# Attention rounds of a decoder trunk: the value products move into the following round

## The chip, the cores and the metric

One core of a Trainium2 chip runs the whole program. The metric is the time of one execution on the device, in microseconds (us), smaller being better.

## What is computed

Two layers of a decoder trunk on 256 tokens of width 1024. Of each layer only the first half matters here: a combined projection and, among other branches, two kinds of attention on its columns.

```python
z = h @ w_in[l] + b_in[l]                       # 8448 columns
# branch A: 16 query heads, 4 key/value heads, window 128, a sink per head
oa = banded_attention(qa, ka, va, A_WINDOW - 1, sinks)
# branch C: 4 heads in each of 3 dilation groups, combined by their softmax weights
oc = sum_g softmax(lse)_g * dilated_group(qc_g, kc_g, vc_g)
merged = gate_a * (oa @ w_proj_a) + gate_b * (ob @ w_proj_b) + gate_c * (oc @ w_proj_c)
x = x + merged @ w_out
x = x + hier_moe(rms_norm(x), ...)              # expert stage, 32 experts
```

## The kernel before, in words

The engines' programs are written out by hand; each engine works through its own list in order and waits on semaphores. The trunk stage of a layer runs `z` as 17 column chunks of 512 (the last 256), each in four items, called convs and numbered j: conv j multiplies two of the eight 128-deep blocks of `h` with their weights, in three passes (high and low parts), 12 matmuls (L1488 to L1490). ScalarE casts the high part of a weight item (`high_at`, L933), VectorE subtracts the low part (`low_half`, L1140), SP loads the items. A chunk's sums stand in two banks, one for each block of 128 tokens, and VectorE adds the bias and copies them out (`z_out`, L1159).

The attention lies between the convs 44 to 67, so that TensorE always has work. It has 12 batches: b below 8 are two query heads of branch A each, b from 8 to 11 are the three groups' heads of branch C. A round b of TensorE (the loop at L1689) holds:

- `gates_conv(44 + 2b)`, into banks 6 and 7
- `scores(b + 1)` (L1611), which VectorE masks and takes the maximum of (`softmax_in`, L1254) and ScalarE turns into exponentials (`exps`, L1016); VectorE divides (`softmax_out`, L1291)
- `pv(b)`: `turn_probs(b)` transposes the probabilities (L1623), then `gates_conv(45 + 2b)`, then the products with the values: `product_pair(b)` (L1639) for b below 8, `products(b)` (L1656) for b = 9, which does batches 8 and 9; nothing for b = 8 and 10. Batch 11's products come later, outside the loop
- `qk(b + 2)`: transposes of the next queries and keys (L1592), where the batch needs new ones: none in rounds 7 and 9

ScalarE's round: `high_at(46 + 2b)`, `pv_out(b)` (L1030, turned probabilities out of banks 3 and 4), `exps(b + 1)`, `o_out(b)` (L1035, the products out of bank 5 into the place of the used queries), `qk_out(b + 2)` (L1009), `high_at(47 + 2b)`. Every product block writes bank 5 and waits until the one before it has been copied out (`o_evac`).

A round with odd b ends a chunk: conv 45 + 2b is its last, and the next conv starts a chunk in the same banks 6 and 7. Its first matmuls for each token block therefore wait for that block's copy on VectorE (`z_evac`); the chunk's convs do token block 1 (bank 7) first, and VectorE can take bank 7 while bank 6 is being finished (`z_half`). For b = 7 and 9 a small reduction (`group_max`) stands between the two copies:

```python
z_out(6, c, BANK, c + 1, True, (1,))
if b + 1 >= 8:
    group_max(b + 1)
z_out(6, c, BANK, c + 1, True, (0,))
low_half(46 + 2 * b, BANK if b < 9 else TAIL, 47 + 2 * b, 1)
```

Of the kernel before, what the change touches and what calls it, by code (L numbers as in the profile page):

```python
# [78 lines left out]
def trunk_program(nc, x, positions, norm1_g, w_in, b_in, attn_sinks, sgu_ln_g, sgu_ln_b, w_spatial,  # L79
# [7 lines left out]
    with ExitStack() as whole:  # L87
# [557 lines left out]
        def trunk_stage(l):  # L645
            with ExitStack():
# [4 lines left out]
                BATCHES = 12  # L651
# [21 lines left out]
                def ring_landed(slot, item):  # L673

                    return 16 * (item // 4 + 1 + (slot == 0 and item >= 40))


                def heads(b):
                    return 2 if b < 8 else 3

                def turned_before(b):

                    return 2 * b if b < 8 else 16 + 3 * (b - 8)
# [5 lines left out]
                def t_first(kind, b):  # L689


                    n = sum(qk_banks(i) for i in range(b if kind == "qk" else min(b + 2, BATCHES)))
                    return n + turned_before(max(b - 1, 0) if kind == "qk" else b)
# [20 lines left out]
                def pts_at(u):  # L714

                    return u % 3 if u < 16 else (u - 16) % 6
# [5 lines left out]
                with ExitStack():  # L722
# [189 lines left out]
                    def _(act):  # L912
# [8 lines left out]
                        def high(jj, w, landed, used):  # L921

                            if landed is not None:
                                act.wait_ge(ring_in[(jj // 2) % RING], landed)
                            if used is not None:
                                act.wait_ge(conv_used, used)
                            elif jj >= 64:
                                item_used(act, jj - 2)
                            if jj >= NARROW:
                                act.copy(whi[:, jj % 2, :].rearrange("p (k n) -> p k n", k=4),  # L930
                                         narrow_slot(jj, None)).then_inc(hi_ready, 1)
                                return
                            act.copy(whi[:, jj % 2, 0:2 * w], half_slot(jj, w)).then_inc(hi_ready, 1)  # L933
# [48 lines left out]
                        def high_at(j):  # L982
                            if j >= NARROW:
                                item = NARROW // 2 + j % 2
                                act.wait_ge(ring_in[item % RING], ring_landed(item % RING, item))
                                high(j, BANK, None, None)
                                return
                            high(j, TAIL if 64 <= j < Z_CONV else BANK, ring_landed(j // 2 % RING, j // 2), j - 1 if j < 64 else None)
# [33 lines left out]
                        def pv_out(b):  # L1022
                            for i in range(heads(b)):
                                t, u = t_first("pv", b) + i, turned_before(b) + i
                                act.wait_ge(t_ready, t + 1)
                                if 3 <= u < 19:
                                    act.wait_ge(pv_mm, u - 2 if u < 16 else 16)
                                elif u >= 22:
                                    act.wait_ge(pv_mm, 22)
                                act.copy(pts[:, pts_at(u), :], ps[:, 3 + t % 2, 0:384]).then_inc(t_evac, 1)  # L1030

                        def o_out(b):
                            for p in pairs_of(b):
                                act.wait_ge(pv_mm, turned_before(b + 1))
                                act.copy(o_at(p, 1), ps[:, 5, 0:S].rearrange("p (t c) -> p t c", t=TB)).then_inc(o_evac, 1)  # L1035
# [23 lines left out]
                        for b in range(BATCHES):  # L1059
                            if b == 7:  # L1060
                                halves_at(60)
                            else:
                                high_at(46 + 2 * b)
                            if b == BATCHES - 1:
                                high_at(47 + 2 * b)
                            pv_out(b)
                            if b == 8:
                                qk_out(b + 2, 0, 1)
                            if b == BATCHES - 2:
                                high_at(47 + 2 * b)  # L1070
                            if b + 1 < BATCHES:
                                exps(b + 1)
                            if b < BATCHES - 1:
                                o_out(b)
                            if b + 2 < BATCHES:
                                qk_out(b + 2, 1 if b == 8 else 0)
                            if b < BATCHES - 2:
                                high_at(47 + 2 * b)
                            if b in SPLITS:
                                o_high(SPLITS.index(b))  # L1080
# [377 lines left out]
                    def _(pe):  # L1458
# [103 lines left out]
                        def gates_conv(j, between=None):  # L1562

                            z_conv(j, 6, TAIL if j >= 4 * CHUNKS else BANK, j + 1, between, (1, 0),
                                   2 * (j // 4) if j > 4 * AHEAD else None)
# [32 lines left out]
                        def scores(b):  # L1598
                            src = b if b < 8 else 8 + 2 * ((b - 8) // 2)
                            if src >= 8:  # L1600
                                turn_taken(t_first("qk", src) + 1)
                            turn_taken(t_first("qk", src) + qk_banks(src) - 1)
                            if b >= 1:
                                pe.wait_ge(s_free, b)

                            for i, tb in SIDE_BY_SIDE[0:2 * heads(b)]:
                                r = HD * (i if b < 8 else (b + i) % 2)
                                rows = slice(r, r + HD)
                                q = qkt[rows, b % 2, 0:S] if b < 8 else qkt[rows, i, 0:S]
                                k = qkt[rows, 0 if b < 8 else i, S:2 * S]  # L1610
                                mm = pe.matmul(ps[:, i, tb * P:tb * P + (tb + 1) * P], q[:, tb * P:(tb + 1) * P],  # L1611
                                               k[:, 0:(tb + 1) * P], start=True, stop=True)
                                if tb:
                                    mm.then_inc(s_ready, 1)

                        def turn_probs(b, *which):
                            pe.wait_ge(p_ready, 2 * b + 1)
                            for c in range(3):
                                if c == 1:
                                    pe.wait_ge(p_ready, 2 * b + 2)  # L1620
                                for i in which:
                                    bank = bank_for(t_first("pv", b) + i)
                                    mm = pe.transpose(ps[:, bank, c * P:(c + 1) * P],  # L1623
                                                      probs[:, b % 2, i, c * P:(c + 1) * P], ident[:])
                                    if c == 2:
                                        mm.then_inc(t_ready, 1)
# [34 lines left out]
                        def pv(b, between=None):  # L1661
                            if between:
                                turn_probs(b, 0)
                                between()
                                turn_probs(b, 1)
                            else:
                                turn_probs(b, 0, 1)
                            gates_conv(45 + 2 * b, (lambda: turn_probs(b, 2)) if b >= 8 else None)
                            if b < 8:
                                product_pair(b)  # L1670
                            elif b % 2:
                                products(b)
# [16 lines left out]
                        for b in range(BATCHES - 1):  # L1689
                            gates_conv(44 + 2 * b, (lambda: qk(b + 1, 2, 3)) if qk_banks(b + 1) == 3 else None)  # L1690
                            if b == 0:
                                pe.wait_ge(z_evac, 2 * AHEAD)
                                qk(1)
                                pv(b, lambda: scores(1))
                            else:
                                scores(b + 1)
                                pv(b)
                            if b + 2 < BATCHES:
                                qk(b + 2)
# [927 lines left out]
```

## Time and profile before

| what | value |
|---|---|
| median of 3 runs | 1018.7 us (1018.06 to 1020.11) |
| profiled execution | 1018.59 us, its span 1016.9 us |
| mean granted TensorE clock of that span | 0.985 |
| busy in the span: TensorE, VectorE, ScalarE | 951.8, 560.8, 431.0 us |
| attention rounds | about 128 to 230 us and 630 to 732 us |

The span runs from the first to the last instruction. Engines: PE is TensorE's matmul, PEld its weight loads, DVE VectorE, ACT ScalarE. Matmuls are pipelined, and the ends of their records are modelled; distances between their starts are what a block costs.

### The profile page before, as it was taken

What the parts mean: (1) busy time and instruction counts of PE and PEld (TensorE: products, weight loads), DVE (VectorE), ACT (ScalarE), POOL (GpSimd) and SP (SyncE); (2) the same over time, 40 slices, a digit from 0 to 9 for tenths busy, and PEclk for the clock granted to TensorE, in tenths of its full rate; (3) what the DMA queues carried; (4) which work ended last, traced back from release to release, by engine and by line L of the source; (5) the groups of instructions that cost most, each with busy time, mean ns of one, the idle gap of its engine ahead of it and who ended that gap; (6) DMA issues with size and microseconds to landing.
All of it is one profiled execution on the core that took longest, in us unless ns stands there. A gap on an engine that the chain in (4) does not pass through costs nothing.

```text
span 1016.9 us, 15601 instructions
## 1 busy us (share of the span) xinstructions
PE 951.8 (94%) x5898; PEld 665.8 (65%) x5898; DVE 560.8 (55%) x1328; ACT 431.0 (42%) x920; POOL 58.6 (6%) x74
## 2 busy tenths in 40 slices
PE   9999999999999995976999999999999999977787
PEld 7888877778886441532588888777888954434333
DVE  7666787786883332220276668788868634122212
ACT  5434666766444120210363455666764441111122
POOL 1120400000010000000003004000000100000000
PEclk9999999999999998998999999999999999999989
DMA  9975644248999999999997756342599999999996
GB/s 351 348 244 191 193 138 125 83 123 321 361 391 398 422 426 423 426 427 426 418 392 239 239 180 201 125 125 64 174 355 345 406 418 413 425 425 425 426 427 273
DMA packets 97114, 313.03 MB, mean 308 GB/s; under 512 B 13424, under 2 KB 18576, under 8 KB 74512
## 3 DMA queue, kind: packets, MB, share of 16 engines
q1 hardware_dynamic: 96704, 312.04, 80.3%
q8 instruction: 44, 0.72, 0.3%
q14 instruction: 30, 0.25, 0.1%
q10 hardware_dynamic: 336, 0.02, 0.0%
HBM read 310.20 MB, written 1.84 MB: 307 GB/s over the span
## 4 chain that ended last, share of the span: by engine, by line
PE 76%; DMA 13%; SPq 7%; DVE 2%; ACT 1%; issue 1%; POOL 0%; DVEq 0%; POOLq 0%
PE ps L1488 16%; PE ps L1490 15%; PE ps L1489 15%; SPq L505 7%; PE ps L2154 6%; DMA arena<-in_w_expert_up_dram 5%; DMA arena<-in_w_expert_gate_dram 3%; DMA ring_rest<-in_w_expert_up_dram 3%; DMA ring_rest<-in_w_expert_down_dram 3%; PE ps L2128 2%; PE ps L1611 2%; PE ps L1513 2%; PE ps L2228 2%; PE ps L1623 2%; PE ps L2240 2%; PE ps L2099 1%
## 5 line engine op out<-in xcount | busy, mean ns | idle before, releaser
L1140 DVE TENSOR_TENSOR split_w<-arena,split_w 128x512 fp32r<-128x512 f32 (+1 forms) x352 | 232.9, 700 | 101.1 <-ACT split_w L933 97.6
L1488 PE MATMUL ps<-split_w,split_a 128*128 128x512 f32 (+1 forms) x736 | 283.9, 386 | 0.1
L1490 PE MATMUL ps<-split_w,split_a 128*128 128x512 f32 (+1 forms) x736 | 277.1, 376 | 0.0
L1489 PE MATMUL ps<-split_w,split_a 128*128 128x512 f32 (+1 forms) x736 | 276.7, 376 | 0.0
L933 ACT CAST split_w<-arena 128x1024 fp32r<-128x1024 f32 (+1 forms) x171 | 175.8, 1031 | 176.9 <-PE ps L1490 170.0
L1488 PEld LDWEIGHTS ps<-split_w,split_a 128*128 128x128 f32 x736 | 138.5, 188 | 26.6 <-issue 2.2
L1490 PEld LDWEIGHTS ps<-split_w,split_a 128*128 128x128 f32 x736 | 138.4, 188 | 26.0
L1489 PEld LDWEIGHTS ps<-split_w,split_a 128*128 128x128 f32 x736 | 138.7, 188 | 23.5
L2385 DVE SCALAR_TENSOR_TENSOR acts<-ps,wslot,acts 128x256 f32<-128x256 f32 x16 | 7.7, 483 | 171.6 <-ACT acts L2055 148.5
L2154 PE MATMUL ps<-arena,rows 128*32 128x512 f32 x416 | 90.0, 615 | 9.6 <-DMA arena<-in_w_expert_up_dram 6.9
L2154 PE MATMUL ps<-ring_rest,rows 128*32 128x512 f32 x352 | 76.0, 634 | 12.8 <-DMA arena<-in_w_expert_up_dram 12.8
L2055 ACT ACTIVATE acts<-ps,rslot 128x256 f32<-128x256 f32 x16 | 7.6, 474 | 154.0 <-PE ps L2154 149.6
L2128 PEld LDWEIGHTS ps<-arena,work 128*128 128x128 f32 x448 | 52.8, 197 | 28.8 <-issue 24.8
L2128 PE MATMUL ps<-arena,work 128*128 128x128 f32 x448 | 55.8, 283 | 15.6 <-issue 8.9
L2240 PE MATMUL ps<-rows,st 128*128 128x512 f32 x112 | 55.3, 617 | 0.9 <-DVE xs L2366 0.7
L1016 ACT ACTIVATE probs<-probs,neg 128x128 f32<-128x128 f32 x112 | 49.6, 444 | 10.4 <-DVE neg L1264 10.4
L1159 DVE SCALAR_TENSOR_TENSOR arena<-ps,rstd,arena 128x512 f32<-128x512 f32 (+2 forms) x68 | 47.1, 728 | 3.9 <-PE ps L1490 3.7
L2228 PE MATMUL ps<-arena,acts 128*32 128x512 f32 x272 | 43.6, 595 | 5.2 <-ACT acts L2059 5.2
L2154 PEld LDWEIGHTS ps<-arena,rows 128*32 128x32 f32 x416 | 23.6, 113 | 37.1 <-issue 37.0
L2154 PEld LDWEIGHTS ps<-ring_rest,rows 128*32 128x32 f32 x352 | 19.7, 116 | 42.6 <-issue 42.5
L2369 DVE TENSOR_TENSOR xs<-ps,xs 128x512 f32<-128x512 f32 x48 | 33.2, 691 | 18.2 <-PE ps L2240 18.2
L2240 PEld LDWEIGHTS ps<-rows,st 128*128 128x128 f32 x112 | 17.7, 189 | 30.5 <-issue 30.5
(284 smaller groups left out, 1074.6 us busy)
## 6 DMA issues: line engine op xcount, KB each, us to landing
arena<-in_w_in_dram SPq DMA_DIRECT2D x62, 1024.0 KB, 5.3
arena<-in_w_expert_down_dram SPq DMA_DIRECT2D x36, 1024.0 KB, 19.5
arena<-in_w_expert_gate_dram SPq DMA_DIRECT2D x34, 1024.0 KB, 23.9
arena<-in_w_expert_up_dram SPq DMA_DIRECT2D x32, 1024.0 KB, 24.0
ring_rest<-in_w_expert_down_dram SPq DMA_DIRECT2D x24, 1024.0 KB, 17.4
ring_rest<-in_w_expert_gate_dram SPq DMA_DIRECT2D x22, 1024.0 KB, 23.9
ring_rest<-in_w_expert_up_dram SPq DMA_DIRECT2D x22, 1024.0 KB, 25.5
arena<-in_w_proj_a_dram SPq DMA_DIRECT2D x8, 1024.0 KB, 5.1
```

Of the source, the lines that this page charges most:

```text
L505: sp.dma_start(slot, w[l, 4 * n + e].rearrange("(p k) f -> p (k f)", p=P)).then_inc(done, 16)
L933: act.copy(whi[:, jj % 2, 0:2 * w], half_slot(jj, w)).then_inc(hi_ready, 1)
L1016: act.activation(probs[:, i, n, lo:hi], probs[:, i, n, lo:hi], ACT.Exp, bias=neg[:, i, tb, n:n + 1], accum_out=den[:, i, tb, n:n + 1])
L1140: dve.tensor_tensor(wlo[:, jj % 2, cols], half_slot(jj, w)[:, cols], whi[:, jj % 2, cols].bitcast(F32), ALU.subtract).then_inc(low_split i ...
L1159: dve.scalar_tensor_tensor(out=z[:, tb, cols], in0=ps[:, bank + tb, 0:w], scalar=rstd[:, tb:tb + 1], in1=z[:, 0, cols], op0=ALU.mult, op1= ...
L1488: pe.matmul(o, hi, rhs_hi, start=first, stop=False)
L1489: pe.matmul(o, hi, rhs_lo, start=False, stop=False)
L1490: return pe.matmul(o, lo, rhs_hi, start=False, stop=last)
L2128: mm = pe.matmul(ps[:, 4 + k // 4, (k % 4) * QUAD:(k % 4 + 1) * QUAD], work[:, tb, k * P:(k + 1) * P], onehot[:, n % 2, tb, :], start=(tb ...
L2154: mm = pe.matmul(ps[e * EC:(e + 1) * EC, n % 2, :].rearrange("p (a f) -> p a f", a=2), xsel[:, k, e * EC:(e + 1) * EC], w, start=(k == 0), ...
L2228: mm = pe.matmul(ps[e * EC:(e + 1) * EC, 2 + nh, :], at_sb[:, kf, e * EC:(e + 1) * EC], w, start=(kf == 0), stop=(kf == 1), skip_group_che ...
L2240: pe.matmul(ps[:, 4 + tb, :], st[:, n % 2, tb * P:(tb + 1) * P], y[:, nh * BANK:(nh + 1) * BANK], start=True, stop=True).then_inc(R.back_r ...
```

## The change

The products of a batch are issued in the following round, directly behind that round's scores and ahead of its turned probabilities. ScalarE copies bank 5 out ahead of its copies of the turned probabilities of that round. Round 0 has no products, round 8 has pair 7, round 10 the products of batches 8 and 9.

```diff
--- before.py
+++ after.py
@@ -1063,6 +1063,8 @@
                                 high_at(46 + 2 * b)
                             if b == BATCHES - 1:
                                 high_at(47 + 2 * b)
+                            if b >= 1:
+                                o_out(b - 1)
                             pv_out(b)
                             if b == 8:
                                 qk_out(b + 2, 0, 1)
@@ -1070,8 +1072,6 @@
                                 high_at(47 + 2 * b)
                             if b + 1 < BATCHES:
                                 exps(b + 1)
-                            if b < BATCHES - 1:
-                                o_out(b)
                             if b + 2 < BATCHES:
                                 qk_out(b + 2, 1 if b == 8 else 0)
                             if b < BATCHES - 2:
@@ -1666,6 +1666,8 @@
                             else:
                                 turn_probs(b, 0, 1)
                             gates_conv(45 + 2 * b, (lambda: turn_probs(b, 2)) if b >= 8 else None)
+
+                        def products_of(b):
                             if b < 8:
                                 product_pair(b)
                             elif b % 2:
@@ -1694,6 +1696,7 @@
                                 pv(b, lambda: scores(1))
                             else:
                                 scores(b + 1)
+                                products_of(b - 1)
                                 pv(b)
                             if b + 2 < BATCHES:
                                 qk(b + 2)
```

## Rows read from the trace of the kernel before

**Rows 1.** The page: the chain that ended last, shares of the span by engine.
```profile
PE 76%; DMA 13%; SPq 7%; DVE 2%; ACT 1%; issue 1%; POOL 0%; DVEq 0%; POOLq 0%
```

**Rows 2.** Table of stages, round 2: stretch, length, busy and count per engine, clock, DMA.
```profile
152.30:160.90 8.60, 8.60 (x51) 6.36 (x51) 6.37 (x20) 5.78 (x15) 0.00 (x0) 1.00 0.40 124
```

**Rows 3.** Timeline of TensorE, round 2: start, length, engine, line, operation, operands, count.
```profile
152.30 0.93 PE L1611 MATMUL ps<-qkt 64*128 64x128 f32 x8
153.16 0.87 PE L1623 MATMUL ps<-ident,probs 128*128 128x128 f32 x6
153.79 0.48 PE L1488 MATMUL ps<-split_w,split_a 128*128 128x512 f32 x1
...
156.41 0.39 PE L1490 MATMUL ps<-split_w,split_a 128*128 128x512 f32 x1
156.73 0.87 PE L1639 MATMUL ps<-mixed,arena 128*64 128x256 f32 x8
157.53 0.33 PE L1592 MATMUL ps<-ident,arena 128*128 128x128 f32 x1
...
157.94 0.49 PE L1488 MATMUL ps<-split_w,split_a 128*128 128x512 f32 x1
```

**Rows 4.** Timeline of TensorE: transposes of batch 0 directly behind conv 41.
```profile
124.87 0.39 PE L1490 MATMUL ps<-split_w,split_a 128*128 128x512 f32 x1
125.10 0.27 PE L1592 MATMUL ps<-ident,arena 128*128 128x128 f32 x1
...
125.45 0.48 PE L1488 MATMUL ps<-split_w,split_a 128*128 128x512 f32 x1
```

**Rows 5.** The chain of waits: scores of three heads, start and time on the chain.
```profile
195.75 1.50 PE ps L1611 x12
```

**Rows 6.** Timeline of ScalarE and VectorE, round 2: brackets hold the wait before.
```profile
157.67 0.37 ACT L1035 COPY arena<-ps 128x256 f32<-128x256 f32 x1 [0.63 <-PE ps L1639]
159.79 1.29 DVE L1140 TENSOR_TENSOR split_w<-arena,split_w 128x512 fp32r<-128x512 f32 x2 [1.28 <-ACT split_w L933]
```

**Rows 7.** Timeline, end of round 1: VectorE's two copies, TensorE's conv 47 and 48.
```profile
147.80 1.43 DVE L1159 SCALAR_TENSOR_TENSOR arena<-ps,rstd,arena 128x512 f32<-128x512 f32 x2 [0.55 <-PE ps L1490]
148.06 0.39 PE L1490 MATMUL ps<-split_w,split_a 128*128 128x512 f32 x1
149.37 0.48 PE L1488 MATMUL ps<-split_w,split_a 128*128 128x512 f32 x1
```

**Rows 8.** Timeline, end of round 7: the two copies, and conv 59 and 60.
```profile
200.24 0.74 DVE L1159 SCALAR_TENSOR_TENSOR arena<-ps,rstd,arena 128x512 f32<-128x512 f32 x1
200.46 0.39 PE L1490 MATMUL ps<-split_w,split_a 128*128 128x512 f32 x1
201.16 0.74 DVE L1159 SCALAR_TENSOR_TENSOR arena<-ps,rstd,arena 128x512 f32<-128x512 f32 x1
201.57 0.50 PE L1488 MATMUL ps<-split_w,split_a 128*128 128x512 f32 x1
```

**Rows 9.** Timeline, round 9: a weight load that waits for VectorE's division.
```profile
215.16 0.95 DVE L1291 TENSOR_TENSOR probs<-probs,den 128x768 f32<-128x768 f32 x1
216.17 0.42 PEld L1623 LDWEIGHTS ps<-ident,probs 128*128 128x128 f32 x4 [0.39 <-DVE probs L1291]
```

**Rows 10.** Timeline, end of round 9 and conv 64: copies, products, conv, scores.
```profile
219.51 0.75 DVE L1159 SCALAR_TENSOR_TENSOR arena<-ps,rstd,arena 128x512 f32<-128x512 f32 x1
220.10 2.17 PE L1656 MATMUL ps<-mixed,arena 128*64 128x256 f32 x24
220.45 0.74 DVE L1159 SCALAR_TENSOR_TENSOR arena<-ps,rstd,arena 128x512 f32<-128x512 f32 x1
222.21 0.38 PE L1488 MATMUL ps<-split_w,split_a 128*128 128x256 f32 x1
222.67 0.28 PE L1488 MATMUL ps<-split_w,split_a 128*128 128x256 f32 x1
223.83 1.57 PE L1611 MATMUL ps<-qkt 64*128 64x128 f32 x12
```

## The prediction

> **What bounds the kernel now.** I read four views, in this order. The page's chain of waits says who sets the end: TensorE holds 76% of it, DMA 13% [rows 1]. The table of stages, cut at the starts of the score blocks, says that in the attention rounds TensorE is busy for the whole of a round (8.60 of 8.60 us in round 2) at a granted clock of 1.00 (2.4 GHz), while VectorE has 6.37 and ScalarE 5.78 us of work [rows 2]. So a round costs what TensorE's queue costs, plus what TensorE waits for. The timeline of TensorE then gives the price of each block, start to start, and that of VectorE gives the moments at which banks 6 and 7 come free. All rounds of one parity look alike and layer 2 repeats layer 1, so a few rows stand for all.
>
> **Prices of the blocks** (round 2) [rows 3]: scores 0.86 (152.30 to 153.16), turned probabilities 0.63 (to 153.79), product pair 0.80 (156.73 to 157.53), four transposes for the next queries and keys 0.41 (to 157.94). The products begin 0.32 after the start of the last projection matmul (156.41 to 156.73). Where transposes follow a projection block directly, the step is only 0.23 and four of them take 0.35 [rows 4].
>
> **The change, part by part.** It adds and removes no instruction. It moves nine blocks of products per layer (pairs 0 to 7 and the three-head block issued for batch 9) from the end of their round to the place between the scores and the turned probabilities of the next round; and nine copies of bank 5 on ScalarE, from behind the exponentials to ahead of the copies of the turned probabilities. SP's and POOL's queues are untouched; their waits are on counts that this order reaches in the same sequence.
>
> *Transitions on TensorE.* No row shows scores followed by products. Nearest are scores followed by full-array transposes, which have the 0.86, and products followed by them, which have the 0.80 [rows 3]. I take both unchanged. At the old place the projection block now runs straight into the transposes: 0.32 becomes 0.23 and 0.41 becomes 0.35, a gain of 0.15 in a round that has them.
> Bounds of the unknown step: a score block of three heads holds the chain 1.50 [rows 5] and one of two 0.86, so a third head alone costs about 0.64 and two side by side would cost that as well if nothing drained; the drain behind scores is then about 0.21. The new step can save that 0.21 (no second drain) or pay it twice. Over 18 places that is -3.8 to +3.8 us; I take 0, as the rows nearest by kind have it, and half of it on each side for the range.
> The Trainium skill (TensorEngine Tiling (Array Packing), Key Properties) says that changing the tiling mode drains TensorE. By it a round has four such changes before (into and out of scores, into and out of products) and three after, one fewer; the entries on which this shows cost 0.09 here [rows 3, 4], which is in the sum already; at the 0.21 estimated for a drain behind scores the 18 places would give back another 2.2 us.
>
> *Round 0* issues no products any more: -0.80 and -0.15.
>
> *Rounds 2, 4, 6* exchange one pair for the other: -0.15 each, -0.45. For ScalarE: the copy of bank 5 waited 0.63 for the products, behind the exponentials [rows 6]; now it and the two copies of the turned probabilities stand ahead of them and the exponentials end about 0.6 later. That lies beside TensorE's next block; VectorE waited 1.28 there for the next weight half [rows 6], which ScalarE still casts at the same distance from the transposes. Were that cover gone, each such round would pay what exceeds it.
>
> *Rounds 1, 3, 5*: here the next projection block starts a new column chunk in banks 6 and 7, which VectorE must have emptied. Its two copies start at 147.80 and the following block at 149.37 [rows 7]: the products (0.80) and two transposes stood between. In the new order the whole projection block, and so the first copy, comes 0.80 later: 148.60, plus 0.74 for one copy [rows 8], is 149.34. A weight load that waits for VectorE starts 0.06 after its end (215.16 + 0.95 = 216.11, then 216.17) [rows 9], so 149.40, where the clean order would give about 149.25 (148.06 + 0.80 + 0.23 + two transposes at 0.09). The second copy ends 0.7 later, the second stationary group needs it 0.8 later: not late. So these rounds lose what they gained: +0.05 each, +0.15.
>
> *Round 7* has no transposes at its end, so the new chunk would follow at once: 200.46 + 0.80 + 0.23 = 201.49. The copies, 0.92 apart because a small maximum stands between them [rows 8], come: first 201.00 to 201.74 (it waits for the matmul 0.69 ahead of the last, 199.77 + 0.80 + 0.39), so TensorE starts at 201.80; second 201.92 to 202.66, so the second group starts at 202.72 instead of the natural 202.58. Before, that group followed the start at 201.57 by 0.78, at 202.35; the block ends 0.4 later than before: +0.40, where the clean order had won 0.2.
>
> *Round 8* receives pair 7: +0.80.
>
> *Round 9* loses the three-head products, 2.11 (220.10 to 222.21), and has again no transposes. The clean start of the next block is 220.10 - 0.32 + 0.23 = 220.01. VectorE's copies begin at 219.51 and 220.45 [rows 10]; they don't move, since products no longer precede this block in its round. First free at 219.51 + 0.74 + 0.06 = 220.31, second at 220.45 + 0.74 + 0.06 = 221.25. Before, the second group started at 222.67 and the scores 1.16 later, at 223.83 [rows 10]. After: 221.30 + 1.16 = 222.46, -1.37. Of the 2.11 taken away, some 0.9 comes back as waiting.
>
> *Round 10* receives the three-head products: +2.11. Behind it each step keeps its distance from the projection block: the turned probabilities of batch 11 still come at their old distance.
>
> **Sum per layer**: -0.95 + 0.15 - 0.45 + 0.40 + 0.80 - 1.37 + 2.11 = +0.69; two layers +1.4 us. The profiled execution took 1018.6 us (span 1016.9 and 1.7 around it), the median of three runs is 1018.7, so no correction is due. Forecast: 1018.6 + 1.4 = 1020.0. About 0.2% (2.0 us) is what a measurement of this kernel can tell from no change; the forecast is inside it. The late trunk and the expert stage I take as shifted whole: their loads wait for counts behind this stage.
>
> **Rivals.**
> 1. *The bank waits don't bind*, for instance because VectorE gets to its copies sooner than I shift them. Then nine places save 0.15 in each layer, 2.7 us, 1015.9: faster. For it: most rounds have VectorE a fourth idle [rows 2]. Against: in rounds 7 and 9 the copies have a fixed order with the maximum between them and nothing in the change hastens them. Chance 0.12, with the cheaper drain counted in.
> 2. *Two drains in a row* (slower). The products wait for the scores to leave the array and the transposes for the products, and the first of these costs more than 0.86 includes. Place: between scores and products, 18 times. At the full 0.21 extra it costs 3.8 us, 1023.8. It decides from 0.035 each ((2.04 - 1.4) / 18). For it: every change between block kinds shows a step longer than its stream. Against: the 0.86 already holds the drain of the scores, and the 0.80 that of the products. Chance 0.26.
> 3. *ScalarE's order becomes the bound* (slower): exponentials 0.6 later, then the next weight half late by what exceeds the 1.28; 0.3 in each of five rounds and both layers is 3 us on top of the forecast, 1023.0. Against: ScalarE does 5.78 of 8.60 us, and the wait removed (0.63) pays for the 0.6. Chance 0.07.
> 4. *The change moves nothing that counts*: the expert stage takes up the shift, 1018.6. For it: DMA has 13% of the chain [rows 1]. Against: its loads start on counts that shift too. Chance 0.10.
>
> **How the numbers follow.** Forecast 0.45. Rivals 1 to 4 as given. The forecast and rival 4 are inside 0.2%: 0.55. Faster 0.12, slower 0.33. The range takes half of the drain bound (1.9) around the forecast and reaches toward both other sides: 1017.0 to 1022.8.
>
> **What would show it.** In the timeline of the changed kernel: products right behind scores at 0.86, and turned probabilities 0.80 behind those; transposes 0.23 behind the last projection matmul; the blocks behind rounds 7 and 9 waiting on VectorE's copy out of banks 6 and 7, in sum about 0.5 and 0.9 us per layer; round 2 at 8.45, round 9 at about 8.4 instead of 9.76. It is wrong if scores to products is over 0.95 or under 0.75, if those waits are missing, or if ScalarE's weight casts become late.

## Result and profile after

The changed kernel takes 1020.57 us in the median of 11 runs, the kernel before 1018.31 us (12 runs): ratio 1.0019, 95% interval 1.0011 to 1.0027, a loss of 1.1 to 2.8 us. A twelfth run of the changed kernel was a slow one of 1922.65 us and is in none of these figures. The forecast was 1020.0, a loss of 1.4 us; measured are about 2 us.

The page of the changed kernel, its span, TensorE's row, and the chain by engine:

```profile
span 1018.0 us, 15601 instructions
...
PE 957.5 (94%) x5898; PEld 669.7 (66%) x5898; DVE 560.4 (55%) x1328; ACT 430.5 (42%) x920; POOL 58.4 (6%) x74
...
PE 77%; DMA 10%; SPq 7%; DVE 3%; issue 1%; ACT 1%; DVEq 0%; POOL 0%; POOLq 0%
```

The number of instructions is unchanged, and beside TensorE's share of the chain VectorE's grew, from 2% [rows 1] to 3%. The spans of two single executions differ by 1.1 us, which is not the difference of the kernels: the changed one reached its first scores 0.54 us earlier (127.85 against 128.39), ahead of anything that was changed, and took about 0.4 us less between the two attention stages. So I measure inside the stage, from start to start of the score blocks, where single executions repeat within some 0.03 us a round.

The table of stages for rounds 1, 2, 7 and 9 of the changed kernel, columns as in [rows 2]:

```profile
142.44:150.95 8.51, 8.48 (x49) 6.24 (x48) 6.24 (x20) 5.45 (x15) 0.00 (x0) 1.00 0.37 123
150.95:159.41 8.46, 8.46 (x52) 6.44 (x51) 7.02 (x21) 5.77 (x15) 0.00 (x0) 1.00 0.39 126
194.23:203.56 9.33, 9.08 (x51) 6.48 (x50) 8.17 (x28) 6.82 (x21) 0.00 (x0) 1.00 0.21 58
213.88:222.30 8.42, 7.79 (x46) 5.76 (x45) 7.57 (x29) 5.81 (x20) 0.00 (x0) 1.00 0.50 133
```

In round 2 TensorE is still busy throughout; in rounds 7 and 9 it now has 0.25 and 0.63 us without a matmul, at the same granted clock of 1.00. The kernel before had none in round 7:

```profile
195.68:204.56 8.88, 8.88 (x51) 6.56 (x51) 7.67 (x28) 6.71 (x21) 0.00 (x0) 1.00 0.22 61
```

The lengths of all rounds of layer 1, taken from the timelines (us, start of scores(b + 1) to start of scores(b + 2); the last entry runs to the transposes of branch B behind the stage):

| round | 0 | 1 | 2 | 3 | 4 | 5 | 6 | 7 | 8 | 9 | 10 and on | sum |
|---|---|---|---|---|---|---|---|---|---|---|---|---|
| before | 8.28 | 8.35 | 8.60 | 8.35 | 8.60 | 8.36 | 9.47 | 8.88 | 9.51 | 9.76 | 18.73 | 106.89 |
| after | 7.31 | 8.51 | 8.46 | 8.51 | 8.45 | 8.52 | 9.34 | 9.33 | 10.32 | 8.42 | 20.84 | 108.01 |
| difference | -0.97 | +0.16 | -0.14 | +0.16 | -0.15 | +0.16 | -0.13 | +0.45 | +0.81 | -1.34 | +2.11 | +1.12 |
| predicted | -0.95 | +0.05 | -0.15 | +0.05 | -0.15 | +0.05 | -0.15 | +0.40 | +0.80 | -1.37 | +2.11 | +0.69 |

Layer 2 gives +0.99 in the same way (114.15 to 115.14 from its first scores on). Together +2.1 us: the whole difference lies in the two attention stages. Behind the second one the two profiled executions take the same, 272.50 and 272.47 us.

**The new order on TensorE**, round 2 of the changed kernel, timeline with the columns of [rows 3]:

```profile
150.95 0.93 PE L1611 MATMUL ps<-qkt 64*128 64x128 f32 x8
151.81 0.87 PE L1639 MATMUL ps<-mixed,arena 128*64 128x256 f32 x8
152.61 0.88 PE L1623 MATMUL ps<-ident,probs 128*128 128x128 f32 x6
153.24 0.49 PE L1488 MATMUL ps<-split_w,split_a 128*128 128x512 f32 x1
...
155.88 0.39 PE L1490 MATMUL ps<-split_w,split_a 128*128 128x512 f32 x1
156.11 0.27 PE L1592 MATMUL ps<-ident,arena 128*128 128x128 f32 x1
...
156.47 0.48 PE L1488 MATMUL ps<-split_w,split_a 128*128 128x512 f32 x1
```

The steps are 0.86, 0.80, 0.63, and then 0.23 and 0.36: the prices of [rows 3] and [rows 4] in a new sequence. Two changes of tiling in a row cost nothing beyond them.

**Where a chunk ends.** The end of round 1, with VectorE's two copies, to be held against [rows 7]:

```profile
147.11 1.44 DVE L1159 SCALAR_TENSOR_TENSOR arena<-ps,rstd,arena 128x512 f32<-128x512 f32 x2 [1.36 <-PE ps L1490]
147.37 0.39 PE L1490 MATMUL ps<-split_w,split_a 128*128 128x512 f32 x1
147.60 0.38 PE L1592 MATMUL ps<-ident,arena 128*128 128x128 f32 x2
148.01 0.47 PE L1488 MATMUL ps<-split_w,split_a 128*128 128x512 f32 x1
```

The block behind the two transposes starts 0.41 after the first of them. Two transposes take 0.20 behind products (149.17 to 149.37 in the kernel before) and 0.13 directly behind a projection block (649.72 to 649.85 in the kernel with short copies, below), so some 0.27 of it is waiting. The copy of bank 7 ends at 147.11 + 0.74 = 147.85, and the first matmul follows 0.16 later.

The end of round 7, against [rows 8]:

```profile
199.55 0.75 DVE L1159 SCALAR_TENSOR_TENSOR arena<-ps,rstd,arena 128x512 f32<-128x512 f32 x1 [0.68 <-PE ps L1490]
200.48 0.74 DVE L1159 SCALAR_TENSOR_TENSOR arena<-ps,rstd,arena 128x512 f32<-128x512 f32 x1
...
200.45 0.47 PE L1488 MATMUL ps<-split_w,split_a 128*128 128x512 f32 x1 [0.25 <-DVE arena L1159]
201.28 0.50 PE L1488 MATMUL ps<-split_w,split_a 128*128 128x512 f32 x1
201.62 0.39 PE L1489 MATMUL ps<-split_w,split_a 128*128 128x512 f32 x1
```

And of round 9, against [rows 10], where nothing stands between conv 63 and conv 64 any more:

```profile
219.30 0.75 DVE L1159 SCALAR_TENSOR_TENSOR arena<-ps,rstd,arena 128x512 f32<-128x512 f32 x1
219.56 0.40 PE L1490 MATMUL ps<-split_w,split_a 128*128 128x512 f32 x1
...
220.20 0.36 PE L1488 MATMUL ps<-split_w,split_a 128*128 128x256 f32 x1 [0.24 <-DVE arena L1159]
220.24 0.74 DVE L1159 SCALAR_TENSOR_TENSOR arena<-ps,rstd,arena 128x512 f32<-128x512 f32 x1
...
221.03 0.39 PE L1488 MATMUL ps<-split_w,split_a 128*128 128x256 f32 x1 [0.24 <-DVE arena L1159]
221.26 0.28 PE L1489 MATMUL ps<-split_w,split_a 128*128 128x256 f32 x1
```

Both token blocks wait for their bank. The brackets say 0.24 each, but the records' modelled ends hide part of it: by the starts, the first block comes 0.64 after the last matmul of conv 63 where 0.23 is the clean step, and the second 0.83 after the first where 0.46 was [rows 10]. The next matmul then comes 0.23 behind, where 0.12 is the clean step of these narrower blocks (222.67 to 222.79 in the kernel before): a restart behind this wait costs another 0.11. That is 0.41 + 0.37 + 0.11, about 0.9 us in this one place. Round 7 has the same 0.11 (201.28 to 201.62, clean 0.23). Before, TensorE had no wait for L1159 in the attention stage.

### The profile page after: what moved, and what is told of

The parts are those of the page before. It is cut to its first block, busy times and chain, and to the rows that moved or that the text cites. A ratio compares the mean times of both kernels' runs of the same rounds, so it can differ in the third digit from the quotient of the medians.

```text
span 1018.0 us, 15601 instructions
## 1 busy us (share of the span) xinstructions
PE 957.5 (94%) x5898; PEld 669.7 (66%) x5898; DVE 560.4 (55%) x1328; ACT 430.5 (42%) x920; POOL 58.4 (6%) x74
## 4 chain that ended last, share of the span: by engine, by line
PE 77%; DMA 10%; SPq 7%; DVE 3%; issue 1%; ACT 1%; DVEq 0%; POOL 0%; POOLq 0%
PE ps L1488 16%; PE ps L1490 15%; PE ps L1489 15%; SPq L505 7%; PE ps L2157 7%; DMA arena<-in_w_expert_up_dram 5%; DMA ring_rest<-in_w_expert_down_dram 5%; PE ps L2131 3%; PE ps L2231 3%; PE ps L2243 2%; PE ps L1611 2%; PE ps L1513 2%; PE ps L1623 2%; PE ps L2102 1%; PE ps L1639 1%
## 5 line engine op out<-in xcount | busy, mean ns | idle before, releaser
L2131 PEld LDWEIGHTS ps<-arena,work 128*128 128x128 f32 x448 | 56.4, 208 | 28.7 <-issue 24.6
L2131 PE MATMUL ps<-arena,work 128*128 128x128 f32 x448 | 59.3, 295 | 15.5 <-issue 8.7
L1159 DVE SCALAR_TENSOR_TENSOR arena<-ps,rstd,arena 128x512 f32<-128x512 f32 (+2 forms) x68 | 47.2, 728 | 10.1 <-PE ps L1490 9.9
L2405 DVE COPY rows<-ps 128x512 f32<-128x512 f32 x14 | 9.7, 692 | 52.4 <-PE ps L2231 52.4
```

The source lines that it names most:

```text
L1159: dve.scalar_tensor_tensor(out=z[:, tb, cols], in0=ps[:, bank + tb, 0:w], scalar=rstd[:, tb:tb + 1], in1=z[:, 0, cols], op0=ALU.mult, op1= ...
L2131: mm = pe.matmul(ps[:, 4 + k // 4, (k % 4) * QUAD:(k % 4 + 1) * QUAD], work[:, tb, k * P:(k + 1) * P], onehot[:, n % 2, tb, :], start=(tb ...
```

## Experiments

Theory W: TensorE waits for VectorE's copies out of banks 6 and 7, which the moved blocks had covered. Against it theory D, that back-to-back changes of tiling drain more, and theory S, that ScalarE's order or a shift in later stages is the cause.

**The change again.**

> The changed kernel again, beside the kernel before on one chip. Theory W (the bare bank copies: where a round ends a column chunk, TensorE's next projection block waits for VectorE's copies out of banks 6 and 7, and the moved products were what covered them): +2.2 us, ratio 1.002. Theory D (two drains in a row between scores, products and transposes) gives the same here and differs in the next runs.

1020.5 against 1018.45 us, ratio 1.0023 (1.0011 to 1.0035). Its rounds repeat those above: 115.29 and 115.24 us in the two layers, from their first scores to the transposes behind the stage, against 114.17 and 114.15 before. All stage times below are taken between these two points.

**Only the even batches move.** Line numbers of this kernel are 2 higher.

```diff
-                            if b >= 1:
+                            if b >= 1 and b % 2:
                                 o_out(b - 1)
...
+                            if b % 2 and b < BATCHES - 1:
+                                o_out(b)
...
-                                products_of(b - 1)
+                                if b % 2:
+                                    products_of(b - 1)
                                 pv(b)
+                            if b % 2:
+                                products_of(b)
```

> Only the products of batches 0, 2, 4 and 6 move to the next round; those of odd batches stay at the end of their own round, where they cover VectorE's copies. W: nothing waits for the copies, and each of the four moved blocks gives back 0.14 us: -0.6 per layer, -1.1 us against before, ratio 0.9989. D: each of the 8 moved blocks pays the extra drain that was taken as the cause of +2.2 us over 18 blocks: +1.0 us, ratio 1.0010.

1017.52 against 1018.45 us, ratio 0.9988 (0.9977 to 1.0). The interval reaches no change, so it ran once more:

> The kernel with only the products of batches 0, 2, 4 and 6 moved, a second time, since its first interval (0.9977 to 1.0) reached no change. Its trace gave 113.55 us from the first scores to the transposes behind the attention in either layer, against 114.17 and 114.15 before, so W gives -1.2 us, ratio 0.9988; the theory that this is chance gives 1.000.

1017.03 against 1019.48 us, ratio 0.9983 (0.9974 to 0.9993): faster than the kernel before. From the first scores on the first of the two profiled executions takes 113.55 us in each layer, 0.62 and 0.60 less than before, which was the amount expected; the second takes 113.52 and 113.53. Rounds 1 and 2 of the first:

```profile
143.02 0.93 PE L1613 MATMUL ps<-qkt 64*128 64x128 f32 x8
143.88 0.87 PE L1641 MATMUL ps<-mixed,arena 128*64 128x256 f32 x8
144.68 0.88 PE L1625 MATMUL ps<-ident,probs 128*128 128x128 f32 x6
...
148.27 0.87 PE L1641 MATMUL ps<-mixed,arena 128*64 128x256 f32 x8
149.07 0.44 PE L1594 MATMUL ps<-ident,arena 128*128 128x128 f32 x2
...
152.20 0.93 PE L1613 MATMUL ps<-qkt 64*128 64x128 f32 x8
153.05 0.87 PE L1625 MATMUL ps<-ident,probs 128*128 128x128 f32 x6
```

Round 1 has both blocks, one behind the scores and one covering the copies. Theory D, which wanted this kernel slower, falls: the scores of round 1 are followed by products at 0.86, as they are by transposes in round 2 at 0.85 (152.20 to 153.05).

**Only the odd batches move.** The same edit with `b % 2 == 0`.

> Only the products of batches 1, 3, 5, 7 and the three-head block issued for batch 9 move; even ones stay. W: each round that ends a chunk gives back 0.68 us of the 0.80 taken out and the next pays 0.80: +0.12 three times, +0.39 for pair 7, +0.77 for batch 9: +1.5 per layer, +3.0 us against before, ratio 1.0030, more than the whole change. D: 10 of the 18 blocks pay: +1.2 us, ratio 1.0012.

1022.2 us, ratio 1.0032 (1.0019 to 1.0045); 115.90 and 115.87 us from the first scores on, +1.73 and +1.72. Half of the change loses more than the whole. Rounds 1 and 2 take 7.70 and 9.42 (before 8.35 and 8.60): +0.17 for the pair, where 0.12 was expected. By the stages the two halves sum to -1.2 + 3.4 = +2.2 us, the whole change to +2.1.

**The products of pair 7 and batch 9 stay.**

```diff
-                                products_of(b - 1)
+                                if b - 1 not in (7, 9):
+                                    products_of(b - 1)
                                 pv(b)
+                            if b in (7, 9):
+                                products_of(b)
```

(ScalarE's copies follow.)

> The change, but the products of pair 7 and of batch 9 stay at the end of rounds 7 and 9, the two rounds without transposes. W: the two long waits go (about 0.5 and 0.9 us per layer) and what is left is -0.97 in round 0, +0.16 in rounds 1, 3, 5, -0.14 in rounds 2, 4, 6 and +0.80 in round 7: -0.1 per layer, -0.2 us against before, ratio 0.9998. D: 14 of 18 blocks still pay: +1.7 us, ratio 1.0017.

1018.64 us, ratio 1.0000 (0.9989 to 1.0011); from the first scores on 114.00 and 114.02, -0.17 and -0.13. The waits of these two rounds are worth the whole loss: -0.15 here against +1.12 and +0.99.

**A longer occupation of VectorE ahead of the copies**, in both kernels.

```diff
+                                dve.wait_ge(z_half, c + 1 - AHEAD)
+                                dve.bn_stats(stats[:, 0, 0, :], ps[:, 7, 0:384])
                                 z_out(6, c, BANK, c + 1, True, (1,))
```

> The changed kernel with one more VectorE instruction (statistics over 384 columns of bank 7, estimated 0.45 us from the copies' 0.74 for 512) ahead of the two bank copies in each of the five rounds that end a chunk. Its result is not used. W: the copies are bare, so the full length shows five times in each layer: +4.5 us on top of the change, ratio to before about 1.0066. Theory S (the loss comes from ScalarE's order or from a shift in later stages, the copies are hidden): no more than 1 us on top of the change.

> The same additional VectorE instruction in the kernel before. W: products and transposes cover the copies by about 0.5 us or more in rounds 1, 3, 5 and 9 and nearly that in round 7: at most +0.3 us, ratio 1.000 to 1.0003. S: the same as in the changed kernel.

In the changed kernel 1025.85 us, ratio 1.0065 (1.0045 to 1.0085); in the kernel before 1018.56 against 1019.04 us, ratio 0.9998 (0.9986 to 1.001). The instruction in the changed kernel, with the copies behind it, and the waits of TensorE in the attention stage of layer 1:

```profile
147.83 0.57 DVE L1339 BATCH_NORM_STATS2 stats<-ps 128x6 f32<-128x384 f32 x1 [1.36 <-PE ps L1492]
148.31 1.39 DVE L1159 SCALAR_TENSOR_TENSOR arena<-ps,rstd,arena 128x512 f32<-128x512 f32 x2
```

```profile
PE ps L1490 <- DVE arena L1159: 3.1, 6, 0.7
PEld ps L1490 <- DVE arena L1159: 0.8, 2, 0.4
```

(its line 1490 is the changed kernel's 1488). The additional instruction moves the copies by 0.48. Rounds 1, 3, 5, 7 and 9 of layer 1 grow by 0.47, 0.47, 0.47, 0.44 and 0.45: nearly the full price each time. In the kernel before only round 7 grows, by 0.13 and 0.15, as it had the least cover. The same instruction costs 4.7 us in one order (117.58 + 117.56 against 115.29 + 115.14) and 0.2 in the other (114.27 twice against 114.17 + 114.15). That is cover, shown.

**Short copies in layer 2**, in both kernels. They leave out 448 of the 512 columns of each of these copies, so neither kernel computes the whole result.

```diff
-                                z_out(6, c, BANK, c + 1, True, (1,))
+                                z_out(6, c, 64 if l else BANK, c + 1, True, (1,))
```

(and likewise the one for block 0)

> The changed kernel, but in layer 2 the bank copies of the rounds that end a chunk take 64 of 512 columns (this leaves out most of the last chunks' gate columns in that layer), about 0.2 us each instead of 0.74. Layer 1 is as in the change. W: layer 2's waits vanish: 0.2 in rounds 1, 3, 5, about 0.6 in round 7 and 0.9 in round 9, so 2.1 us below the change, ratio to before 1.0001. S: as the change, 1.0020.

> The kernel before with the same narrow copies in layer 2 (the same part left out). W: its copies were covered, so it gains nothing: ratio 0.9998 to 1.0001. S: the same gain as the changed kernel has from it.

Changed kernel 1018.44 us, ratio 0.9996 (0.9986 to 1.0007); kernel before 1018.11 us, 0.9994 (0.9983 to 1.0005). Layer 1, left alone, takes 115.14 us in the changed one; layer 2 takes 113.09 instead of 115.14. Its rounds 1, 3, 5 take 8.23 each, round 7 8.69, round 9 7.72. The kernel before with the same short copies stays at 114.16. So the full copies cost 2.05 us per layer more than the short ones, and with the short ones the move gains 1.07 us. Round 9 of layer 2:

```profile
719.93 0.28 DVE L1159 SCALAR_TENSOR_TENSOR arena<-ps,rstd,arena 128x64 f32<-128x64 f32 x1
720.62 0.28 DVE L1159 SCALAR_TENSOR_TENSOR arena<-ps,rstd,arena 128x64 f32<-128x64 f32 x1
...
720.18 0.40 PE L1490 MATMUL ps<-split_w,split_a 128*128 128x512 f32 x1
720.42 0.30 PE L1488 MATMUL ps<-split_w,split_a 128*128 128x256 f32 x1
...
720.96 0.39 PE L1488 MATMUL ps<-split_w,split_a 128*128 128x256 f32 x1
```

The block starts 0.24 behind the last matmul: the clean step. The second token block still waits: its copy begins only when conv 63 has ended and ends at 720.90, and the block comes 0.54 behind the first instead of some 0.37, with 0.10 more in the step behind it. By this estimate about 0.27 us of waiting is left in round 9, and without any the move would gain about 1.3 us per layer.

**TensorE's order alone.** ScalarE copies bank 5 behind the exponentials again, one batch late.

```diff
-                            if b >= 1:
-                                o_out(b - 1)
                             pv_out(b)
...
                                 exps(b + 1)
+                            if b >= 1:
+                                o_out(b - 1)
```

> The changed kernel with ScalarE's copy of bank 5 back behind the exponentials (now for the batch before), so that TensorE's order alone is changed. W: ScalarE isn't on the path in either order: the same as the change, ratio to before 1.0019 within 0.0006. S: the copy ahead of the turned probabilities delays the exponentials, so this variant takes back a microsecond or more, 1.0010 or less.

1021.49 us, ratio 1.0029 (1.0019 to 1.0038). The median ratio is outside the band I gave, but its interval overlaps that of the change, and its stages take 115.17 and 115.16 us, as the change's (115.29 and 115.14). It takes back no microsecond; S falls as far as the place of this copy is concerned. The experiment tests less than it seems: the exponentials of round 2 begin 3.37 behind the scores here (150.97 to 154.34) and 3.39 in the change (150.95 to 154.34), because in both they stand behind the turned probabilities, which now come 0.80 later. That their lateness costs nothing is shown by round 2 itself, in which TensorE is busy throughout. Whatever separates 1.0029 from 1.0019 is not in the attention stage and was not followed.

**The small maximum behind both copies.**

```diff
                                 z_out(6, c, BANK, c + 1, True, (1,))
+                                z_out(6, c, BANK, c + 1, True, (0,))
                                 if b + 1 >= 8:
                                     group_max(b + 1)
-                                z_out(6, c, BANK, c + 1, True, (0,))
```

> The changed kernel with VectorE's small maximum (group_max) behind both bank copies instead of between them in rounds 7 and 9. W: the second copy comes 0.27 us sooner; in round 9 that shows in full, in round 7 by 0.05, where the natural start is nearly as late: -0.6 us against the change over both layers, ratio to before about 1.0013. S: no change from 1.0020.

1021.18 us, ratio 1.0018 (1.0009 to 1.0027). Round 7 takes 9.26 and 9.27 instead of 9.33 and 9.31, round 9 stays at 8.42. The expected 0.27 of round 9 is missing. Its timeline tells why:

```profile
219.12 1.45 DVE L1159 SCALAR_TENSOR_TENSOR arena<-ps,rstd,arena 128x512 f32<-128x512 f32 x2
...
220.02 0.36 PE L1488 MATMUL ps<-split_w,split_a 128*128 128x256 f32 x1 [0.24 <-DVE arena L1159]
...
220.63 0.38 PE L1488 MATMUL ps<-split_w,split_a 128*128 128x256 f32 x1
220.76 0.42 DVE L1140 TENSOR_TENSOR split_w<-arena,split_w 128x256 fp32r<-128x256 f32 x1
...
221.23 0.19 PEld L1488 LDWEIGHTS ps<-split_w,split_a 128*128 128x128 f32 x1 [0.19 <-DVE split_w L1140]
```

The second token block now starts 0.61 after the first instead of 0.83, but the second half of the weights, which VectorE prepares behind maximum and copies, comes no sooner (220.76; the change has it at 220.90, with its last matmul of conv 63 0.18 later as well), and TensorE waits for that. VectorE's work between the end of one chunk and the weights of the next is one string, and reordering inside it does nothing for its end.

## Why the prediction was right, and by how much it was off

*What bounds the stage*: right. The prices of TensorE's blocks and its waits for two copies give the length of every round, and the stages' +2.1 us lies inside the measured 1.1 to 2.8.

*Transitions*: right. Scores to products 0.86, products to transposes 0.80, 0.15 back where transposes follow the projection block (measured 0.13 to 0.15). The bounds of 3.8 us on either side, which made most of the range, were far too wide; the true value was the nearest row. The Trainium skill (TensorEngine Tiling (Array Packing), Key Properties) says that changing the tiling mode drains TensorE. The new order has one change fewer per round, and the trace agrees in direction: rounds 2, 4 and 6 gain 0.13 to 0.15. It does not show the 0.21 a place that was weighed beside it.

*Rounds 0, 2, 4, 6, 8, 10*: within 0.02 us of the sum each.

*Rounds 1, 3, 5*: right mechanism, the term mis-sized: +0.05 predicted, +0.16 in layer 1 and about +0.13 in layer 2. The mis-sized term is the price of the handover. I took 0.06 from the end of VectorE's copy, from a weight load [rows 9], and let the matmul start there; the matmul starts 0.15 to 0.16 after the copy's end (147.85 to 148.01). Over three rounds and two layers this is 0.6 of the 0.7 us that the sum of +1.4 lacks against the stages' +2.1.

*Round 7*: +0.45 and +0.43 against +0.40; *round 9*: -1.34 and -1.34 against -1.37. Here the second token block decides, as the prediction had it, and its handover of 0.06 (201.22 to 201.28) and 0.05 (220.98 to 221.03) is the size assumed. Two other terms are off. The restart behind that wait costs 0.11 in the next step, which the sum had at nothing. In round 7 the second block of the kernel before starts at 202.39, not at the 202.35 that I worked out, so it is delayed by 0.34 and not by 0.37. In round 9 the second block starts 0.08 sooner after the scores than I had it (7.15 instead of 7.23; my rows gave 221.25 as the moment the bank is free, and I went on with 221.30), and this nearly cancels the 0.11: that the round comes out within 0.03 is in part luck.

*Rival 1* (the waits don't bind) did not happen; the short copies come near to what it would have been, 1.07 us per layer measured and, with the wait that is left in round 9 taken off, an estimated 1.3, where I had priced 1.35. *Rival 2* (two drains) fell by the rows and by the kernel with the even batches. *Rival 3* (ScalarE): the exponentials of round 2 begin at 3.39 behind the scores instead of 2.77 (155.07 before), the 0.6 expected, and TensorE does not wait longer for it. The cause of that 0.6 is not the copy ahead of them: with the copy put back it is 3.37. It is the turned probabilities, which come 0.80 later. *Rival 4* (the expert stage takes up the shift) is not what the runs show: 1.9 us of time by the ratio against 2.1 in the stages, with an uncertainty of 0.8.

The forecast lay within 0.2% of no change, and so does the ratio of 1.0019, but its interval (0.11 to 0.27%) reaches to either side of that bound.

## What to carry to other kernels

A block that looks like pure work on a saturated engine may be the cover of another engine's hand-over; before moving it, list what becomes free or ready while it runs, and move only those blocks under which nothing does. Here that split the change in two halves of opposite sign, and the good half alone (even batches) makes the kernel 0.12 to 0.17% faster than before. An additional dummy instruction on the suspected engine, in both kernels, measures cover directly: 0.2 us in one and 4.7 in the other.

## What the runs showed of the hardware

A matmul that starts a new group behind a wait for VectorE, with nothing queued between, began 0.15 to 0.16 us after the recorded end of the VectorE instruction (147.85 to 148.01, 200.30 to 200.45, 220.05 to 220.20). The next wait of the same kind, 0.8 us later, cost only 0.05 to 0.06 (201.22 to 201.28, 220.98 to 221.03). Counted to the second matmul of the group the two are closer, 0.45 (200.30 to 200.75) and 0.40 (201.22 to 201.62), because the step behind the waiting matmul is 0.30 in the first case and 0.34 in the second, where 0.23 is clean. So a wait that looks like 0.06 costs 0.11 more just behind it. What makes the first one dearer was not tried.
